# Column orders of an up- and a down-projection: three of four quarters stream their columns otherwise

## The reference

```python
D_FF = 11 * D_MODEL // 4          # 5632

def conv_gated_mlp(h, w_up, conv_w, conv_b, w_down):
    gate, up = jnp.split(h @ w_up, 2, axis=-1)
    return (jax.nn.gelu(dwconv_centred(gate, conv_w, conv_b), approximate=True) * up) @ w_down

# at the end of second_block
    x = x + g2 * conv_gated_mlp(modulate(rmsnorm(x, norm2_g[l]), sh2, sc2), *ffn)
    return rmsnorm(x, final_norm_g)
```

## Time and profile before

| what | us |
|---|---|
| two runs | 2170.68 and 2173.65 |
| median of the runs | 2172.16 |
| span of the profiled execution | 2171.5 |
| TensorE's matmuls busy in it | 2132.8 (98%) |
| TensorE's weight loads busy in it | 1987.9 (92%) |
| VectorE busy in it | 1464.8 (67%) |
| ScalarE busy in it | 1037.6 (48%) |

### The profile page before, as it was taken

One profiled execution on the slowest core, in us unless ns is written; L12 is line 12 of the kernel. 1 busy time (PEld: TensorE's weight loads), 2 busy tenths in 40 slices (PEclk: granted clock), 3 DMA queues, 4 the chain that ended last, 5 costly groups with the idle time before them and its releaser, 6 DMA issues.

```text
span 2171.5 us, 38030 instructions
## 1 busy us (share of the span) xinstructions
PE 2132.8 (98%) x16496; PEld 1987.9 (92%) x16496; DVE 1464.8 (67%) x1850; ACT 1037.6 (48%) x1418; POOL 25.0 (1%) x47
## 2 busy tenths in 40 slices
PE   7999999999999999999999999999999999999998
PEld 7989999988999999998788999999999999988886
DVE  7666556666757698696665577789666665555665
ACT  6554334444454465454433455465444444444454
POOL 0000000110000000000000000000000000000000
PEclk9999999999999999999999999999999999999999
DMA  9765655775448878786565655766777775555553
GB/s 326 239 208 195 196 194 176 232 243 162 153 156 263 295 256 267 252 285 223 182 224 166 233 175 192 255 210 229 240 245 240 243 242 195 194 193 190 182 196 112
DMA packets 339156, 470.05 MB, mean 216 GB/s; under 512 B 14797, under 2 KB 312557, under 8 KB 326126
## 3 DMA queue, kind: packets, MB, share of 16 engines
q1 hardware_dynamic: 337838, 466.93, 64.5%
q0 software_dynamic: 1152, 0.70, 0.1%
HBM read 464.80 MB, written 2.10 MB: 215 GB/s over the span
## 4 chain that ended last, share of the span: by engine, by line
PE 91%; DVE 5%; ACT 2%; DMA 2%; issue 1%; SPq 0%; ACTq 0%; DVEq 0%
PE ps L1971 64%; PE ps L1982 11%; PE ps L1990 4%; DVE wlo L1191 2%; PE ps L2002 1%; PE ps L2060 1%; ACT whi L595 1%; DMA raw<-w_branch_dram 1%; PE ps L2321 1%; PE ps L2261 1%; PE ps L2223 1%; PE ps L2255 1%; DVE arena L1257 1%; DMA raw<-w_in_dram 1%; PE ps L1926 1%
## 5 line engine op out<-in xcount | busy, mean ns | idle before, releaser
L1191 DVE TENSOR_TENSOR wlo<-raw,whi 128x1024 fp32r<-128x1024 f32 (+1 forms) x668 | 814.6, 1221 | 661.7 <-ACT whi L595 658.5
L595 ACT ACTIVATE whi<-raw 128x1024 fp32r<-128x1024 f32 (+1 forms) x668 | 706.3, 1058 | 1065.2 <-PE ps L1971 860.5
L1971 PE MATMUL ps<-f_hi,whi 128*128 128x256 f32 x2112 | 422.0, 281 | 1.6 <-DVE f_lo L1835 1.6
L1971 PE MATMUL ps<-f_lo,whi 128*128 128x256 f32 x2112 | 413.8, 277 | 0.0
L1971 PE MATMUL ps<-f_hi,wlo 128*128 128x256 f32 x2112 | 413.5, 277 | 0.0
L1971 PEld LDWEIGHTS ps<-f_hi,whi 128*128 128x128 f32 x2112 | 320.7, 188 | 14.3 <-issue 11.8
L1971 PEld LDWEIGHTS ps<-f_hi,wlo 128*128 128x128 f32 x2112 | 319.9, 188 | 0.0
L1971 PEld LDWEIGHTS ps<-f_lo,whi 128*128 128x128 f32 x2112 | 319.9, 188 | 0.0
L1971 PE MATMUL ps<-phi,whi 128*128 128x256 f32 (+2 forms) x1440 | 300.7, 290 | 0.0
L1971 PE MATMUL ps<-plo,whi 128*128 128x256 f32 (+2 forms) x1440 | 288.4, 281 | 0.0
L1971 PE MATMUL ps<-phi,wlo 128*128 128x256 f32 (+2 forms) x1440 | 288.1, 281 | 0.0
(11 more groups left out here) (380 smaller groups left out, 2595.1 us busy)
## 6 DMA issues: line engine op xcount, KB each, us to landing
raw<-w_in_dram SPq DMA_DIRECT2D x151, 1024.0 KB, 5.9
raw<-ada_w_dram SPq DMA_DIRECT2D x96, 1024.0 KB, 5.0
raw<-ffn_w_up_dram SPq DMA_DIRECT2D x88, 1024.0 KB, 5.0
raw<-ffn_w_down_dram SPq DMA_DIRECT2D x44, 1024.0 KB, 5.2
raw<-w_out_dram SPq DMA_DIRECT2D x32, 1024.0 KB, 5.7
raw<-w_branch_dram SPq DMA_DIRECT2D x16, 1024.0 KB, 6.1
arena<-xT_dram SPq DMA_DIRECT2D x4, 544.0 KB, 6.6
arena<-ctxT_dram SPq DMA_DIRECT2D x1, 2048.0 KB, 11.1
```

The costliest lines, as they stand in the source:

```text
L595: nc.scalar.activation(whi[slot_of(c)][:, 0:w], src, ACT.Copy).then_inc(S("split_hi"), 1)
L1191: v.tensor_tensor(wlo[slot_of(c)][:, 0:w], src, whi[slot_of(c)][:, 0:w].bitcast(F32), ALU.subtract).then_inc(S("split_lo"), 1)
L1971: l = mm(ps[2 * p + h][0:m, b:b + tt.stop - tt.start], wx[:, k], x[:, xi, tt], start=first, stop=last)
```

## The change

A function order(v, q) gives a view of a row of columns in another order, by the number of the quarter, q. Quarter 0 keeps the running order. Quarter 1 takes pairs apart: columns 0, 1, 4, 5, 8, 9 and so on, and then 2, 3, 6, 7 and so on. Quarter 2 takes runs of 32 in turn from the first and the second half of the row. Quarter 3 takes pairs in turn from the first and the second half. The moving operand and the sums go through the same view, so the product of a column is added where it was before. It is applied at line 1971 for the units of L that are not early, and at line 1982; not in down_last.

```diff
+        def order(v, q):
+
+            if q == 1:
+                return v.rearrange("p (n two r) -> p two n r", two=2, r=2)
+            if q == 2:
+                return v.rearrange("p (two run n) -> p run two n", two=2, n=32)
+            if q == 3:
+                return v.rearrange("p (two n r) -> p n two r", two=2, r=2)
+            return v
...
-                                l = mm(ps[2 * p + h][0:m, b:b + tt.stop - tt.start], wx[:, k], x[:, xi, tt], start=first, stop=last)
+                                moving, sums = x[:, xi, tt], ps[2 * p + h][0:m, b:b + tt.stop - tt.start]
+                                if name == "L" and not early:
+                                    moving, sums = order(moving, q), order(sums, q)
+                                l = mm(sums, wx[:, k], moving, start=first, stop=last)
...
-                                l = mm(ps[(4 if name == "M0" else 0) + 2 * t + nb][:, :], x[:, kd, 128 * t:128 * t + 128],
-                                       wx[:, 512 * nb:512 * nb + 512], start=first, stop=last)
+                                moving, sums = wx[:, 512 * nb:512 * nb + 512], ps[(4 if name == "M0" else 0) + 2 * t + nb][:, :]
+                                moving, sums = order(moving, q), order(sums, q)
+                                l = mm(sums, x[:, kd, 128 * t:128 * t + 128], moving, start=first, stop=last)
```

## The result

The changed kernel takes 2421.54 us (median of two runs, 2417.29 and 2425.79) beside 2172.16 before: 1.114 times the time, with a 95% interval of 1.1087 to 1.1197. That is 249.4 us slower. The forecast was 2172.2 us, with a range up to 2320.

The account below looks back on a forecast made before the run. TensorE's stream of matmuls was taken as the bound. The span of 2171.5 us plus 0 for the three orders gave 2171.5, and with the measured median 0.7 above it a forecast of 2172.2 us, range 2160 to 2320.

Parts of the forecast that it names:

- The bound: Late up- and down-projection: TensorE's stream of matmuls bounds the stage, so a change in a matmul's length enters the time one for one.
- The counts: Touched matmuls: 2736 in the up-projection and 756 in the down-projection, 483.1 us in all or 22% of the span.
- Rival (B): Quarter 1 or 3: one order in pairs streams at half rate, 143.4 us more, 2315.6 us; chance 0.12.
- the bound from above: Touched matmuls at the plain fp32 rate: 101.7 or 201.1 ns more each, 430.2 us for three orders, 143.4 for each.
- I take nothing for all three: Quarters 1 to 3 of both projections: the three orders are forecast to cost 0 us, with 16.1 us kept in the range.
- the nearest in kind: Rows of the same 256-column matmul with operands in other buffers: 117.1 ns, 3.8 ns more; only addresses differ; 16.1 us if all paid.
- (A): All three orders cost nothing, at most 16 us, or gain up to 30; pairs stay whole; 2160 to 2200 us; chance 0.66.
- a gain of up to 30 us: Touched matmuls might get faster by up to 30 us; little of it expected while the weight loads are busy throughout.
- (E): A jump costs part of a cycle: pair orders lose 71.7 us or quarter 2's run borders 68.1; about 2242 us; chance 0.09.
- (C): Quarters 1 and 3: both orders in pairs run at half rate, the runs of 32 don't; 2459.0 us; chance 0.07.
- The doubt about the side: If only matmuls get longer, the trace can't tell whether reading the columns or writing the sums costs; no size given.
- The sign to look for in the weight loads: On TensorE: weight loads longer than 188 ns would mean the conflict is on the SBUF side.

## Why the prediction was wrong

What held. The bound: TensorE's stream is the path, and each nanosecond of a matmul came out at the end (ScalarE's waits grew by 248.3 us, the late stage by 248.2). The counts: 2736 and 756 matmuls, one third of them in each quarter. The groups that read f_hi, f_lo, dhi and dlo are the only ones that moved. The granted clock stayed at 1.00 (0.99 in the piece from 1921.35 us).

What came near. Rival (B) has one order at half the rate, and pairs apart do stream at half the rate. But its size went by plain fp32 matmuls and was to be the bound from above; the measured cost is over it: 117 and 224 ns more for a matmul (5.52 us for 24 and 5.44 for 12, less), where the prediction had 101.7 and 201.1. Its reason, steps that meet the same part of the bank each time, is shown by no run: the sums in that order cost nothing (2.72 us for 24 matmuls).

What failed is the step "I take nothing for all three". It went by the earlier trace rows, "the nearest in kind", where operands lie in other buffers. Those rows are of streams in running order, and they can't show the cost of an order. They were also misread as a matter of where operands lie: in the kernel before, line 1971 takes 2.83 us for 24 matmuls at 1107.04 us with f_hi and f_lo, the operands that take 2.72 in the late up-projection, and in the runs of 32 one and the same operand goes from one level to the other. Pairs apart take two columns from each group, visit twice as many groups and pay for each as for a whole one, 230 ns for 113. The runs with aligned and shifted fours show this: 118 and 221 ns for the same length of run. That pairs stay whole, which spoke for (A), is not enough: of the orders tried, only those that take all four columns of a group stay near the running order's 113 ns, at 118 to 127 (three of four was not tried).

Two terms in the forecast's range and rivals were the author's, and no run shows them: a gain of up to 30 us, where no order tried took less than the running order's 113 ns, and the 68.1 us of (E) for the borders of runs, which come back in the expectation for the runs of 32 alone and where 13.2 us were measured.

By terms, from the pieces of the run with the columns alone, over 38 and 21 units. Pairs apart, forecast 0 (B: 143.4 us): (5.52 - 2.72) x 38 + (5.44 - 2.75) x 21 = 106.4 + 56.5 = 162.9 us, 164.4 measured alone. Pairs in turn, forecast 0 (143.4 if halved): (3.96 - 2.72) x 38 + (4.08 - 2.75) x 21 = 47.1 + 27.9 = 75.0 us, 76.6 measured alone. It is 1.5 times and not twice the running order. The cause of the 1.5 stays open. The runs of 32, forecast 0 with up to 68.1 us: (2.85 - 2.72) x 38 + (2.84 - 2.75) x 21 = 4.9 + 1.9 = 6.8 us in their own quarter, 13.2 measured alone, with the running quarters at their upper level. The three make 244.7 us of the 246.2 by which that run was slower. The outcome lies between (B), 2315.6 us, and (C), 2459.0. No rival had the two orders in pairs at two different rates.

The doubt about the side, "the trace can't tell reads from sums", was right for the trace, and the runs with one side at a time settled it: all columns, no sums. The sign to look for in the weight loads was there, if small: their mean grew from 188 ns to some 196 from 1505 us on, and gaps opened; but the gaps say that the loads wait for matmuls, so in this kernel it proves nothing on the side. With one side at a time the sign does go with it: in the up-projection, with the columns alone, the loads of quarter 1 take 203 to 208 ns in the mean and those of quarter 3 193 to 195, with the sums alone all take 187 or 188.

## What to carry to other kernels

Where TensorE's stream is the bound, look at the moving operand of each fp32r matmul by its groups of 16 bytes: count the groups it visits, not the columns. For pairs and fours apart, aligned or not, each visit at four columns' time gives what was measured within 5% (pairs apart: 128 visits x 1.77 ns = 227 ns, measured 230). Whole aligned groups of four were taken apart for 118 ns in place of 113 and in turn for 127; a view that passes over two of the four at each step doubles the matmul, and so does one that takes fours apart from column 2 on. Where two parts take turns in pairs the count is too high: 1.46 to 1.50 times was measured and not twice. If columns must be permuted, try it where the sums go: six orders that keep aligned pairs were free in PSUM here (2172.65 us beside 2173.99 and 2170.82 beside 2173.64).

## What the runs showed of the hardware

- Reading a group of 16 bytes for a pair of fp32r columns costs 230 / 128 = 1.80 ns, where the pair takes 113.3 / 128 = 0.89 in running order. In the up-projection steps of four, six and eight columns are nearly alike (230, 224 for 252 columns, 233 ns).
- Pairs in turn cost 1.46 times the running order for two parts (165 ns, and 170 or 1.50 in another run), 1.50 for three parts of 82 columns (163 ns) and 1.64 for three of 80 (174 ns), and twice for four and eight parts (230 ns). With 512 columns four parts take 446 ns and eight 495. The cause of these levels is not shown.
- Runs in turn from both halves get cheaper slowly with their length: 127 ns for four, 123 for eight, 119 for 32 columns. The first was run with the sums reordered too.
- The sums' order cost nothing in three quarters of each of two runs (2.72 us for 24 matmuls and 2.75 for 12, as before), with steps from four columns to a half of the row, though each matmul adds to what is there.
- A matmul in running order has two levels, 113 and 118 ns, with the same operands. Runs of 32 in one quarter move the running quarters behind it from one to the other, which by the estimate above is 6.3 of the 13.2 us. Aligned fours apart (118 ns) are no slower than a running order at its upper level.
